# A float32r weight ring kept word by word, and matmuls that walk their stream and their output backwards

## The chip, the cores and the metric

The kernel runs on one core of one Trainium2 chip. The metric is the device time of one execution in microseconds (us): the median of three runs is 1799.5 us (1799.42 to 1800.07).

## The reference

One layer of a streaming encoder on x of 512 frames by 1024 features, float32:

```python
h = h + 0.5 * swiglu(rmsnorm(h, ffn1_norm), w_gate, w_up, w_down)            # FFN_DIM 2816
u = rmsnorm(h, mix_norm)
h = h + (sigmoid(gate_0) * (gla(u) @ w_branch_gla)       # gated linear attention, 4 heads
       + sigmoid(gate_1) * (ssd(u) @ w_branch_ssm)       # Mamba-2 scan, 8 groups, causal convolution
       + sigmoid(gate_2) * (attention(u) @ w_branch_attn)) @ w_out   # own chunk and 8 before
h = h + 0.5 * swiglu(rmsnorm(h, ffn2_norm), ...)
y = rmsnorm(h, final_norm)
```

q, k, v, the gates, z and so on are columns of one product `u @ w_in`. Nearly all arithmetic is in these dense products: per pass over the 512 frames, 297 slabs of weights, each 128 partitions by 1024 words.

## The kernel before

**Precision.** TensorE multiplies float32r, a rounded float32. To keep the precision of float32, each operand is split into a rounded part (H) and a remainder (L), and a product is three: H by H, L by H, H by L. Activations are kept in pairs (UH/UL, NH/NL, HH/HL, SH/SL, GH/GL, AH/AL, MH/ML), weights in WH/WL.

**The weight ring.** SyncE loads one slab of 512 KB at a time into `RAW[:, slot, :]` (three slots, line 401). ScalarE rounds it into WH (`hi`, line 1137, 128x1024 words), VectorE writes the remainder RAW - WH into WL (`lo`, line 1657). `hi` of slab n + 3 waits until TensorE is done with slab n (`slab_done`), `lo` waits for `hi`, the next load into the RAW slot waits for `lo`, and TensorE waits for `lo` of its slab (`need_slab`). Slots 0 and 1 of the rounded parts are one tile, WH01, slot 2 is WH2; WL01 and WL2 hold the remainders. `slab(W, n)` gives the 1024 words of a slab.

**Two kinds of product.** A feature-major product has a block of the slab, 128 by 128 words, as the stationary operand and streams 512 columns of activations: `mm(dst, slab(W, n)[:, k*P:(k+1)*P], R[:, k, :])`, 24 matmuls for a slab (8 blocks, three products). These are issued by `blocks` (line 546), `fm_piece` (566), `fm_fresh` (579 to 582), `fm_first` (593 to 600), `output_part` (868) and, for the last output tile in two halves of 256 columns, `last_half` (673). A token-major product (`tm_tile`, line 613; z, v, r and the attention's v) has activations as the stationary operand and streams 256 columns of the slab. Of the 297 slabs, 40 are token-major. The trace has 6006 feature-major matmuls of 512 columns, 132 of 256 columns, and 1920 token-major ones of 256 columns.

**Addresses.** All activation tiles that are streamed begin 128 bytes past a multiple of 512 bytes in their partition. Unused tiles (`gap0` to `gap2`) put every feature-major slot at the same remainder; a token-major slab begins 16 words later (`TM_LATER`), 64 bytes. LR, which is streamed against WGK in four matmuls (line 930), begins at a multiple of 512 bytes, WGK 128 bytes past one.

**Order.** Each engine's program is written out by hand: first SwiGLU, the small projections, eight rounds of the scan (SSM) with the projections of the next round between its steps, first merge, four rounds of GLA, four of attention, second merge, w_out, second SwiGLU, the last norm. The engines meet by semaphores alone.

Of the kernel before, what the change touches and what calls it, by code (L numbers as in the profile page):

```python
# [18 lines left out]
F32R = mybir.dt.float32r  # L19
# [3 lines left out]
P = 128  # L23
T = 512
D = 1024
KT = D // P
# [3 lines left out]
CH = 64  # L30
# [4 lines left out]
HS = NG * HPG  # L35
# [6 lines left out]
SLAB = 1024  # L42
RING = 3
TM_LATER = 16
LR_ROWS = 96


# [104 lines left out]
def build(nc, a, out):  # L152

    ctx = ExitStack()
    with ctx:
        def sb(name, shape, dt=F32, stack=None):
            return (stack or ctx).enter_context(nc.sbuf_tensor(name, shape, dt))
# [4 lines left out]
        UH = sb("UH", [P, KT, T], F32R, r)  # L162
        UL = sb("UL", [P, KT, T], F32R, r)
# [4 lines left out]
        r.close()  # L168
        SH = sb("SH", [P, 2 * NG, T], F32R)
        RAW = sb("RAW", [P, RING, SLAB])  # L170
        WH01 = sb("WH01", [P, 2 * SLAB + TM_LATER], F32R)
        causal = sb("causal", [P, CH])
        half_gate_bias = sb("half_gate_bias", [P, 3 * KT])
        sb("gap0", [P, 112 - CH - 3 * KT])
        WH2 = sb("WH2", [P, SLAB + TM_LATER], F32R)
        minus_a = sb("minus_a", [P, HS])
        gconv = sb("gconv", [P, 24])
        minus_half = sb("minus_half", [P, 8])
        var4 = sb("var4", [P, 8])
        rstd4 = sb("rstd4", [P, 8])  # L180
        ggrp = sb("ggrp", [P, 8])
        sb("gap1", [P, 112 - HS - 24 - 32])
        WL01 = sb("WL01", [P, 2 * SLAB + TM_LATER], F32R)
        sb("gap2", [P, 112])
        WL2 = sb("WL2", [P, SLAB + TM_LATER], F32R)
        WH, WL = (WH01, WH2), (WL01, WL2)
        cst = sb("cst", [P, NCST])
        ident = sb("ident", [P, P])
        ones = sb("ones", [P, P])
# [1 line left out]

        LR = sb("LR", [LR_ROWS, T], F32R)
        late = ExitStack()
# [11 lines left out]
        gate_th = ut  # L205
        wgk_raw = ut[0:LR_ROWS, 2, :]
        WGK = sb("WGK", [LR_ROWS, 512], F32R, early)
        rms = sb("rms", [P, T], F32, early)
# [97 lines left out]
        G = ctx.enter_context(nc.psum_tensor("G", [P, 3, T], F32))  # L306
# [49 lines left out]
        def token_major(n):  # L356

            for base, rounds, places in ((N_SSM, NG, (4, 5)), (N_GLA, HG, (1, 2, 4, 5)), (N_ATT, NQ, (4, 5))):
                if base <= n.k < base + 6 * rounds:
                    return (n.k - base) % 6 in places  # L360
            return False

        def slab(W, n):

            o = SLAB * (n.slot % 2) + (TM_LATER if token_major(n) else 0)
            return W[n.slot // 2][:, o:o + SLAB]

        def update(c):

# [159 lines left out]
        @block.tensor  # L529
        def _(pe):  # L530
            mm = nc.tensor.matmul
            pe.wait_ge(consts, 1)
            for _ in range(WARM):
                mm(I2[:, 0:P], ones[:], ones[:], start=True, stop=True)
# [3 lines left out]
            def need_slab(n):  # L538
                pe.wait_ge(split_lo, n.value + 1)

            def blocks(dst, n, k0, k1, RH, RL, begin, end):

                ins = None
                for which, (W, R) in enumerate(((WH, RH), (WH, RL), (WL, RH))):
                    for k in range(k0, k1):
                        ins = mm(dst, slab(W, n)[:, (k - k0) * P:(k - k0 + 1) * P], R[:, k, :],  # L546
                                      start=begin and which == 0 and k == k0,
                                      stop=end and which == 2 and k == k1 - 1)
                return ins
# [5 lines left out]
            def fm_piece(dst, n, RH, RL, piece, fresh=False):  # L555

                if fresh and piece == 0:
                    pe.wait_ge(second_hi, 1)
                if fresh and piece == 1:
                    pe.wait_ge(split_hi, n.value + 1)  # L560
                if piece == (4 if fresh else 0):
                    need_slab(n)
                which, k0 = piece // 2, piece % 2 * 4
                W, R = ((WH, RH), (WH, RL), (WL, RH))[which]
                for k in range(k0, k0 + 4):
                    ins = mm(dst, slab(W, n)[:, k * P:(k + 1) * P], R[:, k, :], start=piece == 0 and k == 0,  # L566
                             stop=piece == 5 and k == KT - 1)
                if piece == 5:
                    ins.then_inc(slab_done, 1)

            def fm_fresh(dst, n, stage, source=(UH, UL, uh_ready, ul_ready), before=None):

                RH, RL, hi_ready, lo_ready = source
                need_slab(n)
                for k in range(KT):
                    if before is not None and k == KT - 2:
                        before()
                    pe.wait_ge(hi_ready, 8 * stage + k + 1)
                    mm(dst, slab(WH, n)[:, k * P:(k + 1) * P], RH[:, k, :], start=k == 0, stop=False)
                    mm(dst, slab(WL, n)[:, k * P:(k + 1) * P], RH[:, k, :], start=False, stop=False)  # L580
                    pe.wait_ge(lo_ready, 8 * stage + k + 1)
                    ins = mm(dst, slab(WH, n)[:, k * P:(k + 1) * P], RL[:, k, :], start=False, stop=k == KT - 1)
                ins.then_inc(slab_done, 1)

            def fm_first(dst, n):

                for k in range(KT):
                    if k == 0:
                        pe.wait_ge(first_hi, 1)
                    elif k == FIRST_PIECE:  # L590
                        pe.wait_ge(split_hi, n.value + 1)
                    pe.wait_ge(uh_ready, k + 1)
                    mm(dst, slab(WH, n)[:, k * P:(k + 1) * P], UH[:, k, :], start=k == 0, stop=False)
                    if k == 0:
                        pe.wait_ge(first_lo, 1)
                    elif k == FIRST_PIECE:
                        need_slab(n)
                    mm(dst, slab(WL, n)[:, k * P:(k + 1) * P], UH[:, k, :], start=False, stop=False)
                    pe.wait_ge(ul_ready, k + 1)
                    ins = mm(dst, slab(WH, n)[:, k * P:(k + 1) * P], UL[:, k, :], start=False, stop=k == KT - 1)  # L600
                ins.then_inc(slab_done, 1)

            def tm_tile(n, wn, j, thirds=range(3), source=(NH, NL)):
# [60 lines left out]
            def last_half(half_no, steps):  # L664

                n0 = N_DOWN2 + 3 * (KT - 1)
                dst = (I01[:, T:T + 256], I34[:, 0:256])[half_no]
                for c, which in steps:
                    n, (k0, k1) = At(n0 + c), DOWN_K[c]
                    need_slab(n)  # L670
                    W, R = ((WH, HH), (WH, HL), (WL, HH))[which]
                    for k in range(k0, k1):
                        ins = mm(dst, slab(W, n)[:, (k - k0) * P:(k - k0 + 1) * P], R[:, k, HALVES[half_no]],  # L673
                                 start=(c, which) == (0, 0) and k == 0, stop=(c, which) == (2, 2) and k == k1 - 1)
                return ins

# [75 lines left out]
            def dt_turn():  # L752

                bank_read(At(0))
                for j in range(TT):
                    ins = nc.tensor.transpose(I01[:, j * 32:(j + 1) * 32], dtv[LR_ROWS:P, j * P:(j + 1) * P],
                                              ident[LR_ROWS:P, LR_ROWS:P])
                ins.then_inc(dt_pe, 1)
# [104 lines left out]
            def output_part(n, wn, k0, k1, RH, RL, begin, end, block0=0):  # L863

                for which, (W, R) in enumerate(((WH, RH), (WH, RL), (WL, RH))):
                    for k in range(k0, k1):
                        b = block0 + k - k0
                        ins = mm(G[:, wn.slot, :], slab(W, n)[:, b * P:(b + 1) * P], R[:, k, :],  # L868
                                 start=begin and which == 0 and k == k0, stop=end and which == 2 and k == k1 - 1)
                if end:  # L870
                    ins.then_inc(slab_done, 1)
# [3 lines left out]


            fm_fresh(G[:, 0, :], At(N_SMALL), 1, before=lambda: norm_total(1))
            n, wn = At(N_SSM), At(W_SSM)
            bank_free(wn)
# [29 lines left out]
            n, wn = At(N_MERGE1), At(W_MERGE1)  # L909
# [18 lines left out]
            for hd in range(HG):  # L928
                dst = (I01[:, 0:T], I01[:, T:], I34[:, 0:T], I34[:, T:])[hd]
                ins = mm(dst, WGK[:, hd * P:(hd + 1) * P], LR[:], start=True, stop=True)  # L930
# [5 lines left out]
            with pe.Fori(0, 2) as i:  # L936
                for t in range(3):
                    n, wn = At(N_MERGE1 + 6 + 3 * t, i, 9), At(W_MERGE1 + 4 + 2 * t, i, 6)
# [145 lines left out]
            for q in range(NQ):  # L1084
                for f in range(2):
                    k = 18 * f
# [9 lines left out]
            n, wn = At(N_MERGE2 + 6), At(W_MERGE2 + 6)  # L1096
# [23 lines left out]
        def _(act):  # L1120
# [257 lines left out]
            def ssm_first():  # L1378
# [3 lines left out]
                dt_exp()  # L1382
                nc.scalar.copy(LR[:], dtv[0:LR_ROWS, :]).then_inc(lr_split, 1)
                conv_tanh(0, 0, wn)
# [979 lines left out]
HALVES = (slice(0, 256), slice(256, T))  # L2364
# [129 lines left out]
```

## Time and profile before

| | |
|---|---|
| median of three runs | 1799.5 us |
| span of the profiled execution, first to last instruction | 1798.7 us |
| TensorE matmul busy | 1786.7 us, 99% |
| TensorE weight loads busy | 1506.3 us, 84% |
| VectorE busy | 958.3 us, 53% |
| ScalarE busy | 632.9 us, 35% |
| GpSimd busy | 90.8 us |
| HBM read | 166.21 MB, 94 GB/s over the span |

The span is 0.8 us under the median; the profile gives no other time for its execution. PE is TensorE's matmul row, PEld its weight loads, which run beside matmuls. Matmuls are pipelined: the record of one lasts longer than the distance from its start to the next start, and its end is modelled. So the mean of a matmul's record is not what it costs. What it costs is its pitch, the time from start to start, and that is read from the chain of waits, where a piece of n matmuls in a row has a length.

### The profile page before, as it was taken

To read this page: it belongs to the slowest core of one execution; us is meant where nothing else is said; L and a number is where in the kernel's file an instruction comes from. 1 tells how busy PE (TensorE), PEld (TensorE's weight loads), DVE (VectorE), ACT (ScalarE), POOL (GpSimd) and SP (SyncE) were. 2 spreads that over 40 slices of the span, in tenths; PEclk is the share of its full clock that TensorE was granted. 3 is DMA by queue.
4 is the path that set the end of the run, shared out by engine and by line. 5 is a ranking of instruction groups with operands and counts; after the bars stand their busy time and mean duration, and the time that the engine had idled before them with its cause. 6 is when DMAs were issued, how large, how long until landed. Compare 5 with 4: busy or idle time off the path is not lost.

```text
span 1798.7 us, 26473 instructions
## 1 busy us (share of the span) xinstructions
PE 1786.7 (99%) x10012; PEld 1506.3 (84%) x10012; DVE 958.3 (53%) x1385; ACT 632.9 (35%) x1002; POOL 90.8 (5%) x92
## 2 busy tenths in 40 slices
PE   9999999999999999999999999999999999999998
PEld 7888888888788888888988888888888888888887
DVE  5444443379888888622544446654334544444333
ACT  5322322244444454332333334443222323222221
POOL 2111100000000000000000000000000011111000
PEclk9999999999999999999999999999999999999999
DMA  5323223333233332223222222222222322223332
GB/s 171 105 93 100 98 94 105 106 99 90 83 82 93 87 86 84 82 95 103 94 71 71 93 82 93 90 84 73 102 95 94 103 90 99 93 94 103 106 105 72
DMA packets 53938, 169.30 MB, mean 94 GB/s; under 512 B 6337, under 2 KB 13761, under 8 KB 53873
## 3 DMA queue, kind: packets, MB, share of 16 engines
q1 hardware_dynamic: 45824, 159.15, 27.1%
q10 hardware_dynamic: 8048, 9.24, 2.6%
q8 instruction: 45, 0.74, 0.2%
q14 instruction: 21, 0.16, 0.0%
HBM read 166.21 MB, written 2.16 MB: 94 GB/s over the span
## 4 chain that ended last, share of the span: by engine, by line
PE 97%; DVE 2%; DMA 0%; ACT 0%; issue 0%; POOL 0%; SPq 0%; DVEq 0%; ACTq 0%; POOLq 0%
PE G L546 50%; PE I L546 16%; PE G L613 12%; PE G L566 8%; PE I L1040 1%; PE I L1016 1%; PE I L1006 1%; PE G L868 1%; PE I L673 1%; PE I L808 1%; PE I L817 1%; PE I L827 1%; PE I L794 0%; PE I L976 0%; PE I L980 0%; PE I L778 0%
## 5 line engine op out<-in xcount | busy, mean ns | idle before, releaser
L1657 DVE TENSOR_TENSOR WL<-RAW,WH 128x1024 fp32r<-128x1024 f32 x296 | 372.0, 1260 | 288.7 <-ACT WH L1137 279.4
L1137 ACT CAST WH<-RAW 128x1024 fp32r<-128x1024 f32 x295 | 307.1, 1046 | 223.3 <-PE I L546 126.4
L546 PE MATMUL G<-UH,WH 128*128 128x512 f32 x664 | 164.3, 389 | 0.0
L546 PE MATMUL G<-UL,WH 128*128 128x512 f32 x664 | 164.0, 389 | 0.0
L546 PE MATMUL G<-UH,WL 128*128 128x512 f32 x664 | 164.0, 389 | 0.0
L546 PEld LDWEIGHTS G<-UL,WH 128*128 128x128 f32 x664 | 124.6, 188 | 25.9
L546 PEld LDWEIGHTS G<-UH,WL 128*128 128x128 f32 x664 | 124.6, 188 | 25.9
L546 PEld LDWEIGHTS G<-UH,WH 128*128 128x128 f32 x664 | 124.5, 188 | 25.8
L546 PE MATMUL G<-NH,WH 128*128 128x512 f32 x448 | 114.8, 398 | 0.3 <-ACTq L1291 0.3
L546 PE MATMUL G<-NL,WH 128*128 128x512 f32 x448 | 110.7, 389 | 0.0
L546 PE MATMUL G<-NH,WL 128*128 128x512 f32 x448 | 110.7, 389 | 0.0
L546 PEld LDWEIGHTS G<-NH,WH 128*128 128x128 f32 x448 | 82.5, 189 | 20.5 <-issue 3.8
L546 PEld LDWEIGHTS G<-NL,WH 128*128 128x128 f32 x448 | 84.1, 188 | 17.7
L546 PEld LDWEIGHTS G<-NH,WL 128*128 128x128 f32 x448 | 84.1, 188 | 17.5
L1177 ACT CAST HH<-hid 128x512 f32 (+1 forms) x44 | 27.3, 621 | 168.7 <-DVE hid L1735 168.7
L1173 ACT ACTIVATE hid<-hid 128x512 f32<-128x512 f32 x44 | 27.8, 632 | 164.3 <-DVE hid L1730 164.3
L613 PE MATMUL G<-WH,NH 128*128 128x256 f32 x608 | 85.4, 282 | 0.0
L613 PE MATMUL G<-WL,NH 128*128 128x256 f32 x608 | 84.3, 280 | 0.0
L613 PE MATMUL G<-WH,NL 128*128 128x256 f32 x608 | 83.9, 279 | 0.0
L546 PE MATMUL I<-HL,WH 128*128 128x512 f32 x330 | 82.1, 389 | 0.0
L546 PE MATMUL I<-HH,WH 128*128 128x512 f32 x330 | 82.1, 389 | 0.0
L546 PE MATMUL I<-HH,WL 128*128 128x512 f32 x330 | 82.1, 389 | 0.0
(351 smaller groups left out, 2622.3 us busy)
## 6 DMA issues: line engine op xcount, KB each, us to landing
RAW<-in_slabs SPq DMA_DIRECT2D x296, 512.0 KB, 3.4
cum_rows<-kept_rows ACTq DMA_DIRECT2D x16, 256.0 KB, 6.8
bias<-in_rel ACTq DMA_DIRECT2D x16, 128.0 KB, 2.8
bias<-in_rel ACTq DMA_DIRECT2D x16, 112.0 KB, 2.6
h<-in_x SPq DMA_DIRECT2D x6, 256.0 KB, 6.4
out_y<-h SPq DMA_DIRECT2D x4, 256.0 KB, 2.2
h<-in_x ACTq DMA_DIRECT2D x2, 256.0 KB, 3.5
out_y<-h ACTq DMA_DIRECT2D x4, 128.0 KB, 1.8
```

The source lines that it names most:

```text
L546: ins = mm(dst, slab(W, n)[:, (k - k0) * P:(k - k0 + 1) * P], R[:, k, :], start=begin and which == 0 and k == k0, stop=end and which == 2 ...
L566: ins = mm(dst, slab(W, n)[:, k * P:(k + 1) * P], R[:, k, :], start=piece == 0 and k == 0, stop=piece == 5 and k == KT - 1)
L613: ins = mm(dst, U[:, k, j * P:(j + 1) * P], slab(W, n + k // 4)[:, (k % 4) * 256:(k % 4 + 1) * 256], start=which == 0 and k == 0, stop=whi ...
L673: ins = mm(dst, slab(W, n)[:, (k - k0) * P:(k - k0 + 1) * P], R[:, k, HALVES[half_no]], start=(c, which) == (0, 0) and k == 0, stop=(c, wh ...
L808: ins = mm(I01[s, j * 256 + rr * CH:j * 256 + (rr + 1) * CH], M[s, j, rr, :], XDT[s, j, rr * CH:(rr + 1) * CH], start=True, stop=True)
L817: ins = mm(I34[half(c), (c // 2) * 256:(c // 2 + 1) * 256], CT[:, c * CH:(c + 1) * CH], SS[:, c, :], start=True, stop=True)
L827: ins = nc.tensor.transpose(dst[:, f * T + j * P:f * T + (j + 1) * P], src[:, j, f * P:(f + 1) * P], ident[:])
L868: ins = mm(G[:, wn.slot, :], slab(W, n)[:, b * P:(b + 1) * P], R[:, k, :], start=begin and which == 0 and k == k0, stop=end and which == 2 ...
L1137: nc.scalar.copy(slab(WH, n), RAW[:, n.slot, :]).then_inc(split_hi, 1)
L1173: A(hid[:, t, :], hid[:, t, :], ACT.Silu).then_inc(gate_ready, 1)
L1177: nc.scalar.copy(HH[:, bass.ds(ft, 1), :].rearrange("p a t -> p (a t)"), hid[:, t, :]).then_inc(hh_ready, 1)
L1657: V.tensor_tensor(slab(WL, n), RAW[:, n.slot, :], slab(WH, n).bitcast(F32), ALU.subtract).then_inc(split_lo, 1)
```

## The change

Three things are changed, all for the feature-major products.

1. **One tile for both parts.** Three tiles W0, W1, W2 replace WH01, WH2, WL01, WL2. In a feature-major slab the rounded part and the remainder lie word by word: part H in the even words, part L in the odd ones. ScalarE's write of H, VectorE's read of H and write of L, and TensorE's load of a 128-word block have a step of two words (8 bytes). A block of 128 columns spans 1024 bytes, not 512.
2. **Slots at three distances.** The first word of a feature-major slab lies 0, 32 or 64 words (0, 128, 256 bytes) past the remainder that the streamed tiles have, for slots 0, 1, 2.
3. **Backwards.** `mm_back` gives the streamed tile and the output in PSUM with a step of -1: column 511 comes first and goes to column 511 of the output. What is computed is the same.

A token-major slab keeps its two parts apart inside the slot, 1040 words from one another; its rounded part still begins 16 words in, its remainder now at word 1056, 128 bytes past the remainder of the streamed tiles and not 64. No instruction is added, removed or moved, on any engine; the waits and the DMAs are the same.

```diff
+WOVEN_AT = (0, 32, 64)
+SLOT = 2 * SLAB + 64
...
-        WH01 = sb("WH01", [P, 2 * SLAB + TM_LATER], F32R)
+        W0 = sb("W0", [P, SLOT], F32R)
         causal = sb("causal", [P, CH])
+        W1 = sb("W1", [P, SLOT], F32R)
         half_gate_bias = sb("half_gate_bias", [P, 3 * KT])
-        sb("gap0", [P, 112 - CH - 3 * KT])
-        WH2 = sb("WH2", [P, SLAB + TM_LATER], F32R)
+        gconv = sb("gconv", [P, 24])
+        sb("gap0", [P, 64 - 3 * KT - 24])
+        W2 = sb("W2", [P, SLOT], F32R)
...
-        sb("gap1", [P, 112 - HS - 24 - 32])
-        WL01 = sb("WL01", [P, 2 * SLAB + TM_LATER], F32R)
-        sb("gap2", [P, 112])
-        WL2 = sb("WL2", [P, SLAB + TM_LATER], F32R)
-        WH, WL = (WH01, WH2), (WL01, WL2)
+        sb("gap1", [P, 16])
+        SLOTS = (W0, W1, W2)
+        WH, WL = 0, 1
...
         def slab(W, n):
-            o = SLAB * (n.slot % 2) + (TM_LATER if token_major(n) else 0)
-            return W[n.slot // 2][:, o:o + SLAB]
+            if token_major(n):
+                o = TM_LATER + W * (SLAB + TM_LATER)
+                return SLOTS[n.slot][:, o:o + SLAB]
+            o = WOVEN_AT[n.slot]
+            return SLOTS[n.slot][:, o:o + 2 * SLAB].rearrange("p (c two) -> p c two", two=2)[:, :, W]
+
+        def weights(W, n, b):
+            return slab(W, n)[:, b * P:(b + 1) * P]
...
+            def mm_back(dst, stationary, streamed, start, stop):
+                return mm(dst[:, ::-1], stationary, streamed[:, ::-1], start=start, stop=stop)
...
-                        ins = mm(dst, slab(W, n)[:, (k - k0) * P:(k - k0 + 1) * P], R[:, k, :],
+                        ins = mm_back(dst, weights(W, n, k - k0), R[:, k, :],
                                       start=begin and which == 0 and k == k0,
                                       stop=end and which == 2 and k == k1 - 1)
...
```

The last edit stands likewise in `fm_piece`, `fm_fresh`, `fm_first`, `last_half` and `output_part`; `tm_tile` is as before.

## Rows read from the trace of the kernel before

**Rows 1.** The page: busy time of each engine, and the span in 40 slices.
```profile
PE 1786.7 (99%) x10012; PEld 1506.3 (84%) x10012; DVE 958.3 (53%) x1385; ACT 632.9 (35%) x1002; POOL 90.8 (5%) x92
...
PE   9999999999999999999999999999999999999998
...
DVE  5444443379888888622544446654334544444333
...
PEclk9999999999999999999999999999999999999999
```
**Rows 2.** The page: the chain that ended last, shares of the span by engine.
```profile
PE 97%; DVE 2%; DMA 0%; ACT 0%; issue 0%; POOL 0%; SPq 0%; DVEq 0%; ACTq 0%; POOLq 0%
```
**Rows 3.** The chain's pieces in order of time: start us, length us, what, how many.
```profile
43.09 206.72 PE G L546 x912
249.81 119.68 PE I L546 x528
...
399.14 11.31 PE G L613 x96
...
752.50 0.94 PE I L930 x4
...
1090.03 2.18 PE I L1016 x20
```
**Rows 4.** The chain, 1740 to 1799 us: the last tile in two halves.
```profile
1739.90 32.87 PE I L546 x145
1772.77 9.83 PE I L673 x82
```
**Rows 5.** Groups by form: line, engine, operation, xcount, busy us, mean ns of one.
```profile
L546 PE MATMUL G<-UH,WH 128*128 128x512 f32 x664 | 164.3, 389 | 0.0
...
L546 PEld LDWEIGHTS G<-UH,WL 128*128 128x128 f32 x664 | 124.6, 188 | 25.9
...
L1737 DVE TENSOR_TENSOR HL<-hid,HH 128x512 f32 x39 | 27.0, 692 | 36.1 <-ACT HH L1177 36.1
L1177 ACT CAST HH<-hid 128x512 f32 x42 | 26.1, 621 | 164.4 <-DVE hid L1735 164.4
```
**Rows 6.** Tile RAW: its instructions, duration ns min/median/max, first and last start.
```profile
L1657 DVE TENSOR_TENSOR WL<-RAW,WH x296: 1211/1225/1492, 14.0 to 1773.9; 128x1024 fp32r<-128x1024 f32 x148
L1137 ACT CAST WH<-RAW x295: 1030/1047/1090, 15.8 to 1772.9; 128x1024 fp32r<-128x1024 f32 x148
```
**Rows 7.** Timeline, 60 to 71 us, ScalarE, then VectorE: start us, us, what.
```profile
60.71 1.03 ACT L1137 CAST WH<-RAW 128x1024 fp32r<-128x1024 f32 x1
```
```profile
61.77 1.48 DVE L1657 TENSOR_TENSOR WL<-RAW,WH 128x1024 fp32r<-128x1024 f32 x1 [1.64 <-ACT WH L1137]
```
**Rows 8.** One SSM round, 544 to 586 us, busy us of each engine.
```profile
core 0: us, PE busy (x) PEld busy (x) DVE busy (x) ACT busy (x) POOL busy (x), PEclk, DMA share, GB/s
544.00:586.00 42.00, 42.00 (x323) 36.15 (x321) 36.77 (x53) 20.00 (x36) 2.21 (x2) 1.00 0.32 87
```

More of the change, by code:

```diff
@@ L170, in build @@
         RAW = sb("RAW", [P, RING, SLAB])
-        WH01 = sb("WH01", [P, 2 * SLAB + TM_LATER], F32R)
+        W0 = sb("W0", [P, SLOT], F32R)
         causal = sb("causal", [P, CH])
+        W1 = sb("W1", [P, SLOT], F32R)
         half_gate_bias = sb("half_gate_bias", [P, 3 * KT])
-        sb("gap0", [P, 112 - CH - 3 * KT])
-        WH2 = sb("WH2", [P, SLAB + TM_LATER], F32R)
+        gconv = sb("gconv", [P, 24])
+        sb("gap0", [P, 64 - 3 * KT - 24])
+        W2 = sb("W2", [P, SLOT], F32R)
         minus_a = sb("minus_a", [P, HS])
-        gconv = sb("gconv", [P, 24])
         minus_half = sb("minus_half", [P, 8])
@@ L565, in fm_piece @@
                 for k in range(k0, k0 + 4):
-                    ins = mm(dst, slab(W, n)[:, k * P:(k + 1) * P], R[:, k, :], start=piece == 0 and k == 0,
+                    ins = mm_back(dst, weights(W, n, k), R[:, k, :], start=piece == 0 and k == 0,
                              stop=piece == 5 and k == KT - 1)
@@ L578, in fm_fresh @@
                     pe.wait_ge(hi_ready, 8 * stage + k + 1)
-                    mm(dst, slab(WH, n)[:, k * P:(k + 1) * P], RH[:, k, :], start=k == 0, stop=False)
-                    mm(dst, slab(WL, n)[:, k * P:(k + 1) * P], RH[:, k, :], start=False, stop=False)
+                    mm_back(dst, weights(WH, n, k), RH[:, k, :], start=k == 0, stop=False)
+                    mm_back(dst, weights(WL, n, k), RH[:, k, :], start=False, stop=False)
                     pe.wait_ge(lo_ready, 8 * stage + k + 1)
-                    ins = mm(dst, slab(WH, n)[:, k * P:(k + 1) * P], RL[:, k, :], start=False, stop=k == KT - 1)
+                    ins = mm_back(dst, weights(WH, n, k), RL[:, k, :], start=False, stop=k == KT - 1)
                 ins.then_inc(slab_done, 1)
@@ L592, in fm_first @@
                     pe.wait_ge(uh_ready, k + 1)
-                    mm(dst, slab(WH, n)[:, k * P:(k + 1) * P], UH[:, k, :], start=k == 0, stop=False)
+                    mm_back(dst, weights(WH, n, k), UH[:, k, :], start=k == 0, stop=False)
                     if k == 0:
@@ L597, in fm_first @@
                         need_slab(n)
-                    mm(dst, slab(WL, n)[:, k * P:(k + 1) * P], UH[:, k, :], start=False, stop=False)
+                    mm_back(dst, weights(WL, n, k), UH[:, k, :], start=False, stop=False)
                     pe.wait_ge(ul_ready, k + 1)
-                    ins = mm(dst, slab(WH, n)[:, k * P:(k + 1) * P], UL[:, k, :], start=False, stop=k == KT - 1)
+                    ins = mm_back(dst, weights(WH, n, k), UL[:, k, :], start=False, stop=k == KT - 1)
                 ins.then_inc(slab_done, 1)
@@ L672, in last_half @@
                     for k in range(k0, k1):
-                        ins = mm(dst, slab(W, n)[:, (k - k0) * P:(k - k0 + 1) * P], R[:, k, HALVES[half_no]],
+                        ins = mm_back(dst, weights(W, n, k - k0), R[:, k, HALVES[half_no]],
                                  start=(c, which) == (0, 0) and k == 0, stop=(c, which) == (2, 2) and k == k1 - 1)
@@ L867, in output_part @@
                         b = block0 + k - k0
-                        ins = mm(G[:, wn.slot, :], slab(W, n)[:, b * P:(b + 1) * P], R[:, k, :],
+                        ins = mm_back(G[:, wn.slot, :], weights(W, n, b), R[:, k, :],
                                  start=begin and which == 0 and k == k0, stop=end and which == 2 and k == k1 - 1)
```

## The prediction

> **What bounds the kernel now.** I read the page first. TensorE's matmul row is busy in 1786.7 of 1798.7 us, in every slice of the span; VectorE has 53%, with slices of 8 and 9 tenths between 400 and 650 us, ScalarE 35%; the granted clock is full throughout [rows 1]. The chain of waits agrees: 97% of it is PE, 2% VectorE, nothing DMA [rows 2]. So a change of the matmuls' own pace reaches the end almost whole, and slower weights preparation reaches it only where TensorE would come to wait.
>
> A busy PE row doesn't say that it runs at its peak, since records overlap: a matmul of 512 columns has a record of 389 ns [rows 5]. The pieces of the chain give the pace. 912 feature-major matmuls in a row take 206.72 us and 528 others take 119.68 us: 226.7 ns each, the same for two different streams (UH/UL and HH/HL) and over all three slots [rows 3]. The last output tile has the same matmuls with 256 columns: 82 in 9.83 us, 119.9 ns each [rows 4]. The difference, 106.8 ns for 256 columns, is 0.417 ns for a column, the higher clock level of 2.4 GHz. What is left is no part of the streaming: 226.7 - 213.3 = 13.4 ns, and 119.9 - 106.7 = 13.2 ns. Every feature-major matmul thus pays about 13.3 ns that doesn't depend on how long it streams. One thing happens once for each matmul: the load of the next 128x128 block, whose record lasts 188 ns and lies beside the stream [rows 5].
>
> Two rows say that these 13 ns are not the same everywhere. Token-major matmuls, 256 columns, take 11.31 us for 96: 117.8 ns, that is 11.1 ns over 106.7; their stream begins 64 bytes later. The four matmuls of LR against WGK, 512 columns, take 0.94 us, 235 ns each: 21.7 ns over 213.3; their two operands lie 128 bytes apart, modulo 512 [rows 3]. Four are few, and they have 96 rows, but the price moves with the addresses. I read it as TensorE's two reads of SBUF, the stream and the load beside it, which meet in some part of the memory and hold the stream up. Transposes support that: 20 of them, 128 columns each, take 2.18 us, 109.0 ns, where the load of 128 words at half that clock (0.833 ns a word) is 106.7: they are bound by the load, and the load itself shows at most 2.3 ns on top [rows 3]. So the load isn't held up; the stream is, where it is what counts.
>
> **The change, part by part.** *Word by word, and backwards.* No instruction goes or comes. There are 6006 matmuls of 512 columns and 132 of 256 concerned. Now a load walks 512 bytes in the 106.7 ns in which the stream walks 1024. Afterwards both walk 1024 bytes in that time: equal speeds. If the load takes its block from the last word to the first (no row shows its direction; I assume this one, and the first rival the other), both then walk the same way and keep their distance: either they don't meet, or they meet at the start, the stream is put back a little, and they are apart for the rest. Before, by the same assumption, they walked against each other, and had to pass through each other.
>
> The lower bound for what remains of the 13.3 ns is the 2.3 ns of the transposes: a pitch of 215.6 ns, 11.1 less, 6006 x 11.1 = 66.7 us, and 132 x 11 = 1.5 us. The upper bound is the price of the worst row, LR against WGK, doubled, since a woven block has twice as many bytes to pass: 43 ns, a pitch of 257, +180 us. I take 216.5 ns, near the transposes, as some of the loads of one of the three distances may still meet the stream for a few words. 226.7 - 216.5 = 10.2 ns; 6006 x 10.2 = 61.3 us, and 1.3 us for the 132: 62.6 us off, all on the path.
>
> *The load with a step of two words.* If it took two clocks of its own for each word, 213 ns, it would still lie under a stream of 213.3 ns, and cost only in the 132 short matmuls, 132 x 100 = 13 us at most. I take nothing: the record stays at 188 ns.
>
> *Token-major.* The remainder's stream, 640 of the 1920 matmuls, begins at 128 bytes and not at 64. Bounds: 117.8 - 109.0 = 8.8 ns less (the transposes' floor of the load) or 21.7 - 11.1 = 10.6 ns more (the row of LR): -5.6 to +6.8 us. I take 0.
>
> *ScalarE's and VectorE's accesses with a step.* 296 casts of 1047 ns and 297 subtractions of 1225 ns (up to 1492) [rows 6]. No row shows such a step. From 512 to 1024 columns a cast goes from 621 to 1047 ns, 0.83 ns a column, and a subtraction from 692 to 1225, 1.04 ns [rows 5, 6]; a gain is excluded, since that is one word a clock already. At worst each word takes two clocks: +0.85 us a cast, +1.07 us a subtraction. In SwiGLU that is covered: the cast of a slab starts at 60.71 us, when its slot comes free, and the subtraction ends at 63.25 [rows 7]; TensorE needs the slab two slabs later, 2 x 24 x 0.2267 = 10.9 us after the start, 71.6. The cover of 8 us holds twice the price. In an SSM round it may not: 42.0 us, VectorE 36.77 [rows 8]. With 96 feature-major matmuls the round becomes 41.0 us, and VectorE's margin 4.2 us. At no extra price I count 0.3 us a round for waits that the shorter cover brings out (behind a late `lo` stand VectorE's own steps of the scan, for which TensorE waits), 8 rounds, 2.4 us. At the worst price VectorE has 36.8 + 6 x 1.07 = 43.2 us in a round of 41.0, and if its present idle time of 5.2 us stays, 48.4: +7.4 us a round, 59 us. I take the 2.4 us: a step that keeps two words of a run of four is nearer to a contiguous access than to one word from far apart.
>
> *Sum* for the profiled execution: 1798.7 - 62.6 + 2.4 = 1738.5 us; the median stands 0.8 us over it: 1739 us.
>
> **Two rules weighed.** Rows first: the pitch has 13.3 ns over the stream that change to 11.1 and 21.7 with the operands' places [rows 3, 4]. The Trainium skill, page "SBUF — State Buffer", section "Who interferes with whom", says that TensorE has two independent read ports, for the stream and for weights, that it never waits on anyone, and that only the port pair of VectorE and GpSimd brings contention. By this rule the 13.3 ns are no meeting and stay: 1799 us, the second rival. The three different prices speak against it.
>
> Rows again: a column costs 0.417 ns with an output written upwards [rows 3, 4], and no matmul of this kernel writes downwards. The Trainium skill, page "PSUM — Partial Sum Buffer", in its table of specifications, says that cachelines there have 8 bytes and that any non-contiguous access pattern slows matmuls significantly. If a step of -1 counts as non-contiguous, that is the fourth rival; if two neighbours in a line suffice, in whichever order, nothing is lost.
>
> **The rivals.** *First, slower: the two walks meet more often.* Place: the load beside every feature-major stream. If loads walk upwards, the reversed stream now comes against them at equal speeds, with twice the bytes of a block to pass: 13.3 ns become 26.6. 6006 x 13.3 = 80 us, 1880 us; with waits gone in the SSM rounds nothing comes back. It decides as soon as more than 13.3 ns remain, a pitch over 226.7. For it speaks that the direction is assumed, and that the LR row shows how bad a place can be; against it, that a load in the same direction and at half the speed would before have been overtaken slowly, which should have cost far more than 13.3 ns. A milder form, 3 to 8 ns more (18 to 48 us), belongs here.
>
> *Second, no change.* The 13.3 ns are a fixed price of a float32r load. The equality between both lengths speaks for it, the 11.1 and 21.7 against it. 1799 us.
>
> *Third, it works in one or two of the three slots.* At a fixed distance the walks either never or always meet, so one distance may stay at 226.7 or rise above it. One good slot: 62.6 / 3 = 21 us, 1779 us; two: 42 us, 1758 us. For it: the three slots differ in nothing else. Against: a stream that is held up falls back, and so leaves the place by itself.
>
> *Fourth, slower by far: TensorE's backward stream or output runs at half pace.* Then a column takes 0.833 ns: 6006 x 213 = 1279 us more, 3078 us. Nothing in the trace shows a backward access, for or against.
>
> *Fifth, VectorE becomes the bound of the SSM rounds*, by the worst price above: 1739 + 57 = 1796 us at most, about 1770 in the middle.
>
> **How the numbers follow.** The forecast of a lower pitch in all slots has 0.52, the third rival 0.12, the fifth 0.06, the second 0.07, the first 0.16, the fourth 0.07. What a measurement can tell from no change is 0.2%, 3.6 us. Faster: 0.52 + 0.12 + 0.05 = 0.69. Same: 0.07 + 0.01 = 0.08. Slower: 0.23. The range: at the low end all terms at their bounds, 1799.5 - 68.2 - 5.6 = 1726. Upwards it takes in the third, fifth and second rival and the mild form of the first, 1799.5 + 35 = 1835; above it are the rest of the first, 0.1, and the fourth, 0.07. The forecast's own range is 1726 to 1757 (a pitch of 215.6 to 219.0).
>
> **What would show it.** Right: in the chain of after, the 912 matmuls take about 197.4 us, the 528 about 114.3, the last tile's pieces about 110 ns each; the mean record falls from 389 to some 379 ns; loads stay at 188 ns; casts at 1.05 us and subtractions at 1.22. By slot: the pieces of 8 matmuls between two slabs have one pitch. Wrong: a pitch of 226.7 or more in these pieces (second or first rival), a pitch near 440 (fourth), pieces of two lengths in the rhythm of three slabs (third), or VectorE in the chain of the SSM rounds with its subtraction over 2 us (fifth).

## The result, and the profile after

The changed kernel takes 1839.1 us (1838.89 to 1839.47, three runs) against 1799.5: 1.0219 times the time of before, interval 1.0201 to 1.0238. It is 39.6 us slower. The forecast was 1739, its range 1726 to 1835.

The page of after: span, busy times, the chain's shares. The columns are those of [rows 1, 2].

```profile
span 1837.2 us, 26473 instructions
...
PE 1826.2 (99%) x10012; PEld 1555.6 (85%) x10012; DVE 953.4 (52%) x1385; ACT 662.8 (36%) x1002; POOL 89.8 (5%) x92
...
PEclk9999999999999999999999999999999999999999
...
PE 97%; DVE 2%; ACT 0%; DMA 0%; issue 0%; POOL 0%; SPq 0%; DVEq 0%; ACTq 0%; POOLq 0%
```

Nothing took TensorE's place: the chain is PE to 97% as in [rows 2], at the full clock, and VectorE is less busy in share than before. The pieces of the chain (start us, length us, what, how many) answer to [rows 3]:

```profile
42.84 212.80 PE G L543 x912
255.64 123.20 PE I L543 x528
...
409.21 11.35 PE G L626 x96
...
1410.01 45.28 PE I L543 x192
```

212.80 / 912 and 123.20 / 528 are 233.3 ns, where [rows 3] have 226.7; over a stream of 213.3 ns that is 20.0 ns and not 13.3. The 192 matmuls of w_out have 235.8 ns, and the 640 of the second merge 235.9 (150.95 us). 6006 x 6.67 = 40.0 us; added up over all starts of feature-major matmuls, waits left out, the growth is 40.9 us, and 1.5 us of waits are gone, as the other engines have more time. The span grew by 38.5 us. The whole result is the pitch of the matmuls of 512 columns.

The matmuls of 256 columns in the last tile, changed in the same way, did not get slower. TensorE in after (start us, us, what, how many):

```profile
1812.11 1.12 PE L543 MATMUL I<-HL,W 128*128 128x256 f32 x8
...
1819.99 1.12 PE L543 MATMUL I<-HL,W 128*128 128x256 f32 x8
```

From the first start to the second lie 66 matmuls, 119.4 ns each, where [rows 4] have 119.9. Over a stream of 106.7 ns that is 12.7 ns, and not the 20.0 of 512 columns.

What was feared of the steps of two words shows, off the path. Tile RAW in after (duration ns min/median/max, first and last start), to be held against [rows 6]:

```profile
L1670 DVE TENSOR_TENSOR W<-RAW,W x296: 1214/1226/1381, 13.3 to 1812.7; 128x1024 fp32r<-128x1024 f32 x148
L1150 ACT CAST W<-RAW x295: 1034/1164/1212, 15.2 to 1811.4; 128x1024 fp32r<-128x1024 f32 x148
```

VectorE pays nothing for reading and writing with a step (1226 ns for 1225). ScalarE's cast goes from 1047 to 1164 ns, 0.1 us for each slab, which nobody waits for.

### The profile page after: what moved, and what is told of

Same layout as the page of the kernel before. It is cut to its first block, busy times and chain, and to the rows that moved or that the text cites. A ratio compares the mean times of both kernels' runs of the same rounds, so it can differ in the third digit from the quotient of the medians.

```text
span 1837.2 us, 26473 instructions
## 1 busy us (share of the span) xinstructions
PE 1826.2 (99%) x10012; PEld 1555.6 (85%) x10012; DVE 953.4 (52%) x1385; ACT 662.8 (36%) x1002; POOL 89.8 (5%) x92
## 4 chain that ended last, share of the span: by engine, by line
PE 97%; DVE 2%; ACT 0%; DMA 0%; issue 0%; POOL 0%; SPq 0%; DVEq 0%; ACTq 0%; POOLq 0%
PE G L543 60%; PE I L543 17%; PE G L626 12%; PE I L1053 1%; PE I L1029 1%; PE I L1019 1%; PE I L821 1%; PE I L830 1%; PE I L840 1%; PE I L807 0%; PE I L989 0%; PE I L993 0%; PE I L791 0%; DVE ST L1991 0%; DVE SS L1995 0%; PE I L812 0%
## 5 line engine op out<-in xcount | busy, mean ns | idle before, releaser
L1670 DVE TENSOR_TENSOR W<-RAW,W 128x1024 fp32r<-128x1024 f32 x296 | 366.9, 1242 | 316.9 <-ACT W L1150 314.5
L1150 ACT CAST W<-RAW 128x1024 fp32r<-128x1024 f32 x295 | 337.6, 1150 | 227.4 <-PE I L543 127.6
L543 PE MATMUL G<-UH,W 128*128 128x512 f32 x1440 | 356.0, 398 | 0.6 <-ACT UH L1159 0.6
L543 PEld LDWEIGHTS G<-UH,W 128*128 128x128 f32 x1440 | 282.1, 196 | 54.0 <-ACT W L1366 1.0
L543 PE MATMUL G<-NH,W 128*128 128x512 f32 x1216 | 312.0, 401 | 0.3 <-ACTq L1304 0.3
L543 PEld LDWEIGHTS G<-NH,W 128*128 128x128 f32 x1216 | 235.3, 196 | 48.4 <-issue 4.5
L543 PE MATMUL G<-UL,W 128*128 128x512 f32 x720 | 186.7, 398 | 0.0
L543 PE MATMUL I<-HH,W 128*128 128x512 f32 (+1 forms) x748 | 173.3, 384 | 0.0
L626 PE MATMUL G<-W,NH 128*128 128x256 f32 x1216 | 161.9, 282 | 0.0
L543 PE MATMUL G<-NL,W 128*128 128x512 f32 x608 | 155.4, 399 | 0.0
```

The source lines that it names most:

```text
L543: return mm(dst[:, ::-1], stationary, streamed[:, ::-1], start=start, stop=stop)
L626: ins = mm(dst, U[:, k, j * P:(j + 1) * P], slab(W, n + k // 4)[:, (k % 4) * 256:(k % 4 + 1) * 256], start=which == 0 and k == 0, stop=whi ...
L1150: nc.scalar.copy(slab(WH, n), RAW[:, n.slot, :]).then_inc(split_hi, 1)
L1670: V.tensor_tensor(slab(WL, n), RAW[:, n.slot, :], slab(WH, n).bitcast(F32), ALU.subtract).then_inc(split_lo, 1)
```

## The experiments

In the names, "dense" stands for the slots of before, "woven" for those of the change, and "apart" for the new slots with H and L of a slab one behind the other, so that loads are dense too. Pitches are those of the feature-major matmuls of 512 columns, unless another kind is named.

**Which edit costs.** The changed kernel walked forwards, and the kernel before walked backwards.

```diff
 # woven_fwd, on the changed kernel
-                return mm(dst[:, ::-1], stationary, streamed[:, ::-1], start=start, stop=stop)
+                return mm(dst, stationary, streamed, start=start, stop=stop)
 # dense_back: mm_back as in the change, on the slots of before
 # dense_back_stream: the same with dst and not dst[:, ::-1]
```

> The changed kernel with streams and outputs walked forwards again; the word-by-word slots at their three distances stay. Theory 1 (the 20.0 ns over the stream of the changed kernel are due to the woven load alone, whose steps of 8 bytes touch twice as many 16-byte pieces of memory): the pitch stays at 233.3 ns, 1839 us. Theory 2 (two walks that meet: with both at equal speed the direction decides): forwards the pitch differs from 233.3 by several ns, to about 216 or to 240 and more, 1735 or over 1880 us. Theory 3 (the backward stream or output costs the 6.7 ns): 226.7 ns, 1800 us.

1837.6 us, 1.021 times before (1.0193 to 1.0227). The 912 matmuls take 212.84 us: 233.4 ns on average, by slot 234.4, 231.5 and 234.3. The woven slots alone lose what the change loses, also at distances 0 and 256 bytes (first and third slot).

> The kernel before with streams and outputs walked backwards alone; the slots stay as before. Theory 1 (woven load): 226.7 ns, 1799 us. Theory 2 (meeting): the pitch moves away from 226.7, since the walks of unequal speed now go the other way; which way is open. Theory 3 (backward access costs): 233.3 ns, 1839 us.

1830.6 us, 1.017 times before (1.0153 to 1.0187). Its chain:

```profile
42.90 212.80 PE G L541 x912
255.69 123.20 PE I L541 x528
...
409.25 10.88 PE G L624 x96
```

233.3 ns: the backward walk alone loses it too. In these stretches either edit costs all 6.7 ns, and the two together no more. So neither "the woven load" nor "the backward access" is a price of its own that adds up, and theories 1 and 3 fall. The third row is a surprise: the token-major matmuls, which this kernel issues exactly as before with the same addresses, take 113.3 ns each and not 117.8 [rows 3]. Over the whole kernel the token-major starts add up to 226.6 us, against 232.5 before and after: 5.9 of the 8.5 us by which dense_back is faster than the changed kernel. The second merge and w_out give another 1.9 us: their stretches of 640 and 192 matmuls take 149.53 and 44.80 us here, 150.95 and 45.28 there.

The matmuls of 256 columns have no 20 ns here either:

```profile
1803.63 1.11 PE L541 MATMUL I<-HH,WH 128*128 128x256 f32 x8
...
1812.39 1.11 PE L541 MATMUL I<-HL,WH 128*128 128x256 f32 x8
```

74 matmuls lie between the two starts, 118.4 ns each, 11.7 over the stream. For a backward stream the overhead is thus larger for a long stream, 11.7 ns at 256 columns and 20.0 at 512; forwards it is 13.2 and 13.4 [rows 3, 4].

> The kernel before with only the stream walked backwards; the output in PSUM is written forwards, so each feature-major product comes out with its columns in reverse order. It parts the two backward walks. If the output's direction costs anything, this run is faster than the one with both; if only the stream's direction matters, both have the same pitch. Theory 1: 226.7 ns in both.

1831.2 us (one run), the same 212.80 us for 912. Beside a backward stream the direction of the output in PSUM costs nothing: all of it is the stream's.

**What the overhead hangs on: one side stands still.**

```diff
 # dense_load_still, on the kernel before: the load reads one word 128 times
+                return mm(dst, stationary[:, 0:1].to_broadcast([P, P]), streamed, ...)
 # dense_stream_still: the stream reads one word 512 times
+                return mm(dst, stationary, streamed[:, 0:1].to_broadcast([P, streamed.shape[-1]]), ...)
```

> The kernel before, but each feature-major load reads the first word of its block 128 times (a step of 0), so that the products are wrong. The load takes as long but doesn't walk. Theories 1 and 2 (the 13.3 ns come from what the load touches while the stream runs): the pitch falls to 215.6 to 220 ns, 1733 to 1760 us. If the 13.3 ns are a fixed price of a load, 226.7 ns and 1799 us.

1818.9 us (one run), slower than before: 208.75 us for the 912, 228.9 ns each, and 231.7 ns in the second SwiGLU (233.52 us for 1008). At this place a load that doesn't walk costs more than one that does, though less than the 233.3 ns of the change. So the price does not come from a load that walks past the stream, as theories 1 and 2 had it. That the load's place counts all the same is shown below.

> The kernel before, but each feature-major stream reads its first word 512 times (step 0; products wrong). The stream doesn't walk any more, the load does. If stream and load meet in memory, the pitch changes: to 215.6 to 220 ns if a standing stream needs few reads. If the 13.3 ns belong to the load alone: 226.7 ns.

1734.4 us (one run), 65 us faster than before.

```profile
40.84 196.84 PE G L541 x912
```

196.84 / 912 = 215.8 ns: 2.5 ns over the stream, with the same loads beside it. This is about the pace that I had forecast (216.5), and it takes a stream that goes nowhere.

**Distance.** Slots at other distances from the streams, past the remainder that all streams have.

```diff
 # apart_*: H and L one behind the other in the new slots
-            o = WOVEN_AT[n.slot]
-            return SLOTS[n.slot][:, o:o + 2 * SLAB].rearrange("p (c two) -> p c two", two=2)[:, :, W]
+            o = WOVEN_AT[n.slot] + W * SLAB
+            return SLOTS[n.slot][:, o:o + SLAB]
 # apart_fwd_fine:     WOVEN_AT = (4, 8, 16)      woven_fine: the same on the changed kernel
 # apart_fwd_near:     WOVEN_AT = (60, 48, 2)     woven_one_distance: (0, 0, 0) on the changed kernel
```

> Forward streams, H and L of a slab apart again (loads dense), but the three slots at 0, 128 and 256 bytes past the streams' remainder, as in the change. Theory M (load and stream meet in memory, so their distance counts): slot 0 has 226.7 ns, the two others differ from it and from one another, somewhere in 216 to 240 ns. Theory E (the stream's walk costs by itself, whatever lies beside it): 226.7 ns in all slots, 1799 us.

> The same slots with streams and outputs backwards, loads dense. Theory M: slot 0 has 233.3 ns as in the run with backward streams alone, the others differ. Theory E: 233.3 ns in all slots, about 1831 us.

> The changed kernel with all three slots at distance 0. Theory M: the pitch leaves 233.3 ns, up or down, since for two walks at equal speed in the same direction the distance is all there is. Theory E: 233.3 ns, 1839 us.

> Forward streams, dense loads, the three slots at 16, 32 and 64 bytes past the streams' remainder. Theory M with memory that is divided finely: three different pitches; with memory that is divided at 128 bytes or more: near 226.7 ns in all. Theory E: 226.7 ns in all. Any slot under 226.7 shows where a faster version lies.

> The changed kernel with its slots at 16, 32 and 64 bytes and not at 0, 128, 256. If load and stream in the same direction at equal speed meet only where their distance puts them in the same part of a finely divided memory: at least one slot falls to 216 to 220 ns. If the distance counts for nothing in this direction: 233.3 ns in all three, 1839 us.

> Forward streams, dense loads, slots at 240, 192 and 8 bytes past the streams' remainder. 0 and 256 bytes have 226.7 to 227.2 ns; 16, 32, 64 and 128 have 232.1 to 233.4. If the good place is a point that repeats at 256 bytes: 240 and 192 at 233 ns, and 8 bytes shows how wide it is. Any slot under 226.7 ns is the way to a faster kernel.

What was measured, one run each but for the first kernel, the changed one (three each) and woven_fwd (four); the pitch by slot is the mean distance from start to start in the down projections (HH, HL):

| kernel | load, walk of the stream | distances, bytes | pitch by slot, ns | us |
|---|---|---|---|---|
| before | dense, forwards | 0, 0, 0 | 226.7, 226.7, 226.7 | 1799.5 |
| apart_fwd_distances | dense, forwards | 0, 128, 256 | 226.9, 232.1, 226.7 | 1811.5 |
| apart_fwd_fine | dense, forwards | 16, 32, 64 | 233.4, 233.1, 233.5 | 1835.8 |
| apart_fwd_near | dense, forwards | 240, 192, 8 | 228.3, 229.1, 230.7 | 1812.3 |
| apart_back_distances | dense, backwards | 0, 128, 256 | 233.3, 233.3, 233.3 | 1834.8 |
| changed kernel | woven, backwards | 0, 128, 256 | 233.3, 233.3, 233.3 | 1839.1 |
| woven_one_distance | woven, backwards | 0, 0, 0 | 233.3, 233.3, 233.3 | 1840.8 |
| woven_fine | woven, backwards | 16, 32, 64 | 233.3, 233.3, 233.3 | 1836.3 |
| woven_fwd | woven, forwards | 0, 128, 256 | 234.4, 231.5, 234.3 | 1837.6 |

The slots can be told apart in a timeline of TensorE alone (start us, us, what, how many). In apart_fwd_distances, first SwiGLU, every slab has one row of 8 with UL:

```profile
104.95 1.98 PE L543 MATMUL G<-UL,W 128*128 128x512 f32 x8
106.76 3.79 PE L543 MATMUL G<-UH,W 128*128 128x512 f32 x16
110.39 1.98 PE L543 MATMUL G<-UL,W 128*128 128x512 f32 x8
112.20 3.85 PE L543 MATMUL G<-UH,W 128*128 128x512 f32 x16
115.89 2.02 PE L543 MATMUL G<-UL,W 128*128 128x512 f32 x8
117.75 0.62 PE L543 MATMUL G<-UH,W 128*128 128x512 f32 x2
```

The first two rows of 8 last 1.81 us from start to start, 226 ns each, the third 1.86 us, 232.5 ns: that is slot 1, at 128 bytes. So for a forward stream and a dense load the distance counts. 0 and 256 bytes are the good places, 240, 192 and 8 lie between (228.3 to 230.7 ns), and 16, 32, 64 and 128 have 232 to 233.5. These are means: in the slot at 128 bytes the single pitches go from 228 to 241 ns, in one order that returns with every slab. For a backward stream no distance counts in these products, of six tried with woven loads and three with dense ones, and every single pitch is 233 or 234 ns. So 233 ns is the usual pitch, and the kernel before stood on a place where the overhead is a third lower. No slot had a mean under 226.7 ns.

**Rate or way.** In each of these the stream still has 512 columns and the loads are unchanged.

```diff
 # dense_slow_walk: 256 words, each twice          (woven_slow_walk: the same, backwards, on the changed kernel)
+  streamed[:, 0:streamed.shape[-1] // 2].unsqueeze(2).to_broadcast([P, streamed.shape[-1] // 2, 2])
 # dense_loop_128: 128 words, four times over      (dense_loop_4: 4 words, 128 times over)
+  streamed[:, 0:128].unsqueeze(1).to_broadcast([P, streamed.shape[-1] // 128, 128])
```

> The kernel before with streams of 512 columns that read 256 words, each twice (products wrong): the stream walks forwards at half speed. A standing stream had 215.8 ns. If the price is paid for each part of memory that the stream enters beside a load, half of the 20 ns of the general case stays: 222 to 226 ns. If it is paid once the stream walks at all: 226.7 or 233.3 ns.

> The changed kernel (woven loads, backwards) with streams that read 256 words, each twice (products wrong). If its 20.0 ns are of the same kind as those of the kernel before, a price of rate: 215.8 ns, about 1735 us. If the woven load has a price of its own: over 217 ns.

> The kernel before with forward streams that read the same 128 words four times (products wrong): new words at full rate, a quarter of the way. Price of rate: the overhead stays within 13 to 20 ns over the stream, 226 to 233 ns. Price of distance walked: near 215.8 ns.

> The same with 4 words read 128 times, 16 bytes in all (products wrong). If a stream pays for each read of a word or word pair: 226 to 233 ns. If it pays for each new piece of 16 bytes: 215.8 ns, as the standing stream; unless every return to the first word counts as a new piece.

The first long piece of the chain of each (start us, length us, what, how many), in this order; all four leave out words of the stream, the first two half of them, the third three quarters, the last all but four:

```profile
41.44 196.84 PE G L541 x912
```
```profile
41.36 196.84 PE G L543 x912
```
```profile
42.15 206.72 PE G L541 x912
```
```profile
41.74 196.84 PE G L541 x912
```

At half rate the price is gone, 215.8 ns, in the layout of before (1733.7 us) and in the changed one (1735.9 us, one run each). At full rate over only 512 bytes, four times, it is all there: 226.7 ns, 1797.9 us. At full rate within 16 bytes it is gone again, 215.8 ns, 1735.3 us. So it isn't a matter of how far the stream walks, and at half rate its direction and the woven load don't count either. The price is paid when every column has a new word (0.417 ns), and not when every second column has one, nor when the same four words come round. Between loops of 4 and of 128 words none was tried, so the runs don't show how large the piece of memory is that can be read again for nothing.

**The pace of the token-major products.**

```diff
 # tm_back, on the kernel before (tm_first_back: only where k == 0)
-                        ins = mm(dst, U[...], slab(W, n + k // 4)[:, (k % 4) * 256:(k % 4 + 1) * 256], ...)
+                        ins = mm(dst[:, ::-1], U[...], slab(W, n + k // 4)[:, (k % 4) * 256:(k % 4 + 1) * 256][:, ::-1], ...)
```

> The kernel before with the token-major products alone walked backwards (stream and output). If the pace belongs to the direction of what runs: 1920 matmuls go from 117.8 ns to about 113.3 or to 124 (13.3 or 20 ns over 106.7): 1791 or 1812 us. If their distance of 64 bytes makes the direction indifferent: 1799 us.

1803.7 us, 1.0025 times before (1.0017 to 1.0034): 119.9 ns each in the first 96, where [rows 3] have 117.8. Backwards is slower here too, by 2 ns.

> The kernel before; of every eight token-major matmuls the first walks backwards, the other seven as before. Theory L (a pace, once entered, lasts until something else breaks it): the seven that follow run at 113.3 ns, and the kernel takes 1791 to 1793 us. If each matmul's pace is its own: 1799 us.

1799.8 us, ratio 1.0001 (0.9992 to 1.0009). The first 96 take 11.29 us, 117.6 ns each. The seven that follow a backward one don't go to 113.3 ns, so theory L, as put, is wrong: one backward matmul doesn't bring the pace of 113.3 ns about. Where it stood in dense_back is seen against the kernel before. The chain of before, then that of dense_back:

```profile
489.79 11.51 PE G L613 x96
...
899.05 8.68 PE G L613 x72
...
917.19 8.48 PE G L613 x72
```
```profile
500.17 11.08 PE G L624 x96
...
912.85 8.68 PE G L624 x72
...
931.08 8.16 PE G L624 x72
```

It came after backward products, and in the SSM rounds it held although the scan's small matmuls stand between (first rows; the first matmul of the 96 is late, all starts behind it lie 113.3 ns apart). It was gone behind the transposes and small products of GLA (second rows, as before), and back after the next backward product (third rows). In apart_back_distances, where the remainder's words begin at 128 and not at 64 bytes, the first 16 matmuls after a backward product have it; with the first remainder the pitch goes to 118 ns and stays there. So the same matmuls run at one pace or the other by what ran before them. What brings it about stays open. No kernel that was run and computes the whole result beats the one before.

## Why the prediction was wrong, step by step

- *TensorE's pitch bounds the kernel, and a change of it reaches the end whole.* Right: 6.7 ns more on 6006 matmuls are 40.0 us, and the time grew by 39.6.
- *13.3 ns of each pitch are no part of the streaming, move with the addresses, and belong to reads that get in one another's way.* Right in that it moves: 226.7, 232, 233 ns by distance alone, and 215.8 ns as soon as the stream asks for less. That two reads meet is not shown by it. That the floor is 2.3 to 2.5 ns over the stream was right as well, though no version that streams all its words reached it.
- *The price doesn't depend on how long a matmul streams.* This held for the kernel before and not for the change: 12.7 ns at 256 columns and 20.0 at 512. The term of -1.3 us for the 132 short matmuls should have been about 0.
- *Both walk the same way at equal speed, so they keep their distance and don't meet.* This step failed, and with it the sum. It took the price for that of two walks that pass through each other. The runs show a price that the direction doesn't remove (woven_fwd has 233.4 ns, the changed kernel 233.3), that the distance doesn't remove once the stream goes backwards (233.3 ns at six distances), that a standing load still pays (228.9 to 231.7 ns), and that vanishes at half rate (215.8). A reading that fits, and that no run shows by itself: at full rate the stream has no slack to make up for a read that comes late. The term of -62.6 us should have been +40.0.
- *The kernel before was taken as the bad case, LR's four matmuls as an odd one.* It was the other way round: [rows 3] had LR against WGK at 235 ns, 21.7 over the stream, near the 20 that are usual. Its four starts lie 230, 232, 241 and 233 ns apart, in the range of 228 to 241 that the slot at LR's own distance, 128 bytes, shows in apart_fwd_distances. The 13.3 ns of all the others were the exception, and hung on slots at exactly 0 bytes. The row stood in the text, doubled, as the upper bound, and I chose a value near the other end.
- *The first rival* named the right side and, in its mild form (3 to 8 ns more), the right size, but for its mechanism, twice as many bytes to pass, the runs give nothing: a dense load with a backward stream has the same 233.3 ns. *The second*, a fixed price: wrong, since 215.8 and 233.3 both occur. *The third*, one or two good slots: not in the change, but it is what apart_fwd_distances shows of a forward stream. *The fourth*, from the Trainium skill's page "PSUM — Partial Sum Buffer" (table of specifications: any non-contiguous access pattern slows matmuls significantly): an output with a step of -1 costs nothing, 212.80 us for 912 with it and without, both beside a backward stream. For a step of -1 the measurement decides; no run has a wider step in PSUM. *The fifth*: VectorE's step is free, and ScalarE's costs 0.1 us that is covered.
- *That TensorE never waits on anyone* (the Trainium skill, "SBUF — State Buffer", section "Who interferes with whom"): the runs with other distances and rates move its pitch from 215.8 to 234.4 ns with the same instructions but for their addresses and steps. The page calls TensorE's two read ports independent; a stream that is slower beside some loads than beside others doesn't fit that, though the runs don't show what the two share.
- *The load's record stays at 188 ns*: it is 196 ns in the changed kernel and 188 in dense_back. *Token-major, 0*: their starts add up to 232.5 us before and after. *VectorE's slices of 8 and 9 tenths between 400 and 650 us*: in [rows 1] they reach to about 720 us; nothing in the sum hangs on it. *The 2.4 us of new waits in the SSM rounds*: they were thought of for shorter rounds; the rounds grew longer, and TensorE's waits shrank by 1.5 us in all.
- *The range* ended at 1835. The milder slower case was priced up to 48 us, which is 1847, and the range, said to take it in, added only 35. It missed by 4 us.

**Open.** Why 0 and 256 bytes are good for a forward stream; why a standing load costs 228.9 ns in one SwiGLU and 231.7 in the other; why a backward stream pays 11.7 ns at 256 columns and 20.0 at 512; why some stretches of the changed kernel (w_out, the second merge) sit at 235.8 ns on average and woven_one_distance at 233.3 to 233.7 there, but at 236.7 in 468 matmuls from 769 us on (110.76 us), where the changed kernel has 233.4; what sets the token-major pace. No run leaves the load out, so that it is the load that takes the stream's turn is an inference, from the distances of the forward streams alone. For backward streams, where no distance counts and the overhead is larger for the longer stream, a price of the stream by itself is an untested rival. That loads walk from the last word to the first was assumed and no run shows it: three kernels with the load's words in the opposite order (on the slots of before with the stream forwards and backwards, and on the changed kernel) were written, and none of them gave a time.

## What to carry to other kernels

Before an overhead is explained by what differs between two operands, ask for its general level: if one odd row costs more than all the tuned ones, the tuned ones may be the special case that an edit can only lose. A price by rate is found by cheap runs in which the stream reads each word twice or only four words and so leaves the rest of the operand out: they tell at once whether there is anything to win. A price read off short matmuls need not be that of long ones after a change. With float32r streams of 512 columns as here, the best places were weights at 0 or 256 bytes from the streamed tiles' remainder, dense, with the stream forwards; hold any change of layout against the pitch in the chain of waits.

## What the runs showed of the hardware that was not expected

- A float32r matmul of 512 columns has a pitch of 215.8 ns when its stream reads each word twice or loops over four words, and 226.7 to 234.4 ns, by slot, with a new word in every column, always with a 128x128 load beside it.
- Forwards, that pitch depends on the distance between stream and load: 226.7 ns at 0 and 256 bytes, 233.1 to 233.5 at 16, 32 and 64. Backwards it is 233.3 ns at each distance tried. With 256 columns a backward stream pays 11.7 ns over its columns (dense_back) and not 20.0.
- Token-major matmuls with unchanged operands and addresses have two lasting paces: 117.8 ns [rows 3], and 113.3 after backward products in dense_back, until transposes or small products of GLA come between.
- An output walked backwards in PSUM is free beside a backward stream. So are VectorE's reads and writes with a step of 8 bytes (1225 and 1226 ns for 1024 words); ScalarE's write with that step costs 11% (1047 and 1164 ns).
